# Score matmuls with 128 rows throughout, and chunked attention's query blocks in mixed order

## The chip, the cores and the metric

The kernel runs on one core of a Trainium2 chip. The metric is the device time of one execution in microseconds, from three runs (median). The profile is that of one further execution, taken by the hardware profiler.

## What is computed

Two transformer blocks on 1024 tokens of width 1024, in float32. The first block mixes tokens with three attentions side by side, then has cross attention over 256 memory tokens and a gated feed-forward layer. The second block has a pooling mixer and a sliding-window attention. The parts that matter here are the scores of three attentions with head size 64:

```python
# forget-gate attention ("fox"), 4 heads, causal
sc = einsum('bqhd,bkhd->bhqk', qb, k) * 64 ** -0.5
sc = sc + cum[q] - cum[k]          # cumulated log forget gates, per head
sc = where(k_pos <= q_pos, sc, -inf)

# chunked attention, 4 heads: chunks of 64 queries see their own and 8 chunks before
sc = einsum('bqhd,bkhd->bhqk', qc, kb) * 64 ** -0.5
sc = where(valid, sc + bias, -inf)

# sliding-window attention, 16 query heads on 2 key heads, window 128, with sinks
s = einsum('bnqhgd,bnkhd->bnhgqk', qn, kn) + pos_bias
```

Each is followed by a softmax over the keys and the product with the values. Every attention's output then goes through an RMS norm of its own.

## The kernel before

It is written by hand, engine by engine, with semaphores. A float32 operand of a large product is split into a high and a low part of type float32r, which TensorE takes in one pass each instead of the passes of plain float32: high x high, high x low, low x high (`product`, L489).

Attention is worked in units of one block of 128 queries (t = 0 to 7) and one head. `attention_pe` (L622) goes through the units with scores two units ahead: for each step it transposes the probabilities of unit u (`turn`, L647), makes the scores of unit u + 2 (`scores`, L637) and multiplies the transposed probabilities of unit u - 1 with the values (`weigh`, L659). VectorE takes the maximum of the scores (`maximum`, L693 or, with a bias, L697), ScalarE the exponential (L789); the two share the copies of the transposed probabilities (L714, L797). `att_mix` runs 96 units in one chain: 32 of latent attention (MLA), 32 of fox, 32 of chunked attention, each by query block in rising order, four heads to a block. `att_swa` runs 128 units of sliding-window attention and places between them, one product of 512 columns and three matmuls a step, the projection of the next heads' queries (`swa_beside`).

The scores of the 64-wide heads use a stacked operand: the query's high part in one half of the 128 partitions and its low part in the other (`fox_stack`, `chk_stack`, `swa_stack`), against the key's high part in both halves (`fox_khi`, `chk_khi`, `swa_khi`). That is one matmul of 128 rows. The query's high part against the key's low part (`fox_klo`, `chk_klo`, `swa_klo`) is a second one of 64 rows, since the low part lies in one half alone. Keys are taken in banks of 512 columns (`key_banks`, L828). Where the last bank has only 128 columns, plain float32 operands of 64 rows are used (`fox_q`, `fox_k`, `chk_q`, `chk_k`). In fox a third matmul in bfloat16 adds the forget gates: it takes the 32 rows of its head from `aug_q` and `aug_k`, into which the cumulated gates are laid in three parts. A block of fox ends with the causal mask, a bfloat16 matmul with the identity.

The splits of queries and keys for fox and chunked attention are made on GpSimd (POOL) while the attention before runs (L1191 to L1218), each waiting for the one before it through `half_ready`; TensorE waits for `HALVES` of them at the first unit of fox and for twice that at the first unit of chunked attention (L1388 to L1393). POOL then splits the strips of the next weights. For sliding window the key's high part is made on ScalarE (L1952), its low part on VectorE (L2362), the query stacks on POOL (L1230 to L1240).

Query block t of chunked attention has min(t, 4) + 1 tiles of 128 keys: 1, 2, 3, 4, and 5 for t = 4 to 7. Its outputs go to `ytok`, the sums of squares to `ystat` (L926), and after the last block the rows are scaled (POOL, L1224), transposed (L1405) and multiplied with the output weights.

Of the kernel before, what the change touches and what calls it, by code (L numbers as in the profile page):

```python
# [30 lines left out]
F32 = mybir.dt.float32  # L31
# [6 lines left out]
P = 128  # L38
# [23 lines left out]
HALVES = 5 * HEADS  # L62
# [37 lines left out]
N_CF = C_EPS + 2  # L100
# [5 lines left out]
def build(nc, dram, out):  # L106
    ctx = ExitStack()
    with ctx:
# [39 lines left out]
        def col(name, i=0, n=1):  # L148
# [8 lines left out]
                                              ("chk_klo", [P, HEADS // 2, T], F32R)])  # L157
# [4 lines left out]
        _, swa_klo, swa_bias, p3, pt3 = shared([("x_kept", [P, KEPT, T], F32), ("swa_klo", [P, T], F32R),  # L162
# [14 lines left out]
            ("v4", [P, HEADS, CHK_SPAN], F32), ("v5", [P, 2, T], BF16), ("v6", [P, T], F32), ("fox_norm", [P, 2, T], F32R)])  # L177
        (_, _, _, _, _, _, _, _, mem_raw, mem_hi, mem_lo) = shared([
# [23 lines left out]
        (swa_stack, swa_q, swa_kv, swa_z, swa_khi, swa_v, osb3) = shared([  # L202
            ("swa_stack", [P, 2, 2, T], F32R), ("swa_q", [P, 2, T], F32), ("swa_kv", [P, 2, T], F32),
            ("swa_z", [P, NK, T], F32), ("swa_khi", [P, 2, T], F32R),
            ("swa_v", [P, QT, P], F32), ("osb3", [P, HALF], F32)])
# [643 lines left out]
        def fox_stack(h, t, rows_of=slice(0, P)):  # L849
            if h < 2:  # L850
                return ring(split_hi, h)[rows_of, t * P:(t + 1) * P]
            return fox_rows[rows_of, t, fox_at + (h - 2) * P:fox_at + (h - 1) * P]
# [25 lines left out]
        for t in range(QT):  # L878
            q_tok = slice(t * P, (t + 1) * P)
            first = max(0, t - 4)  # L880
            for h in range(HEADS):
                r = slice(HD * (h % 2), HD * (h % 2) + HD)
# [114 lines left out]
        def stacks_done(tile, half, kv):  # L997
            return 2 * HALVES + 8 * tile + 4 * half + 2 * kv + 2

# [1545 lines left out]
```

## Time and profile before

| | us |
|---|---|
| median of three runs | 2717.97 |
| lowest and highest | 2709.69, 2726.29 |
| the profiled execution | 2709.43 |
| its span, first to last instruction | 2707.6 |
| TensorE matmul busy | 2602.9 (96%) |
| TensorE weight load busy | 2112.7 (78%) |
| VectorE busy | 1271.9 (47%) |
| ScalarE busy | 600.3 (22%) |
| GpSimd busy | 1108.2 (41%) |

The busy time of a matmul reaches from its start to the modelled end of its results; neighbours overlap, so what one costs the stream is read from start to start. TensorE's clock has two levels, 1.2 and 2.4 GHz; the granted clock is the share of full speed in a stretch.

### The profile page before, as it was taken

What the parts mean: (1) busy time and instruction counts of PE and PEld (TensorE: products, weight loads), DVE (VectorE), ACT (ScalarE), POOL (GpSimd) and SP (SyncE); (2) the same over time, 40 slices, a digit from 0 to 9 for tenths busy, and PEclk for the clock granted to TensorE, in tenths of its full rate; (3) what the DMA queues carried; (4) which work ended last, traced back from release to release, by engine and by line L of the source; (5) the groups of instructions that cost most, each with busy time, mean ns of one, the idle gap of its engine ahead of it and who ended that gap; (6) DMA issues with size and microseconds to landing.
All of it is one profiled execution on the core that took longest, in us unless ns stands there. A gap on an engine that the chain in (4) does not pass through costs nothing.

```text
span 2707.6 us, 30776 instructions
## 1 busy us (share of the span) xinstructions
PE 2602.9 (96%) x12086; PEld 2112.7 (78%) x12086; DVE 1271.9 (47%) x1526; ACT 600.3 (22%) x1189; POOL 1108.2 (41%) x507
## 2 busy tenths in 40 slices
PE   6999999999999999999999989999999999999987
PEld 5787777878777888888888867887878787777776
DVE  5247544343545353535352677342535272244465
ACT  3012444221232000000000332010101132344432
POOL 5533661014313444444444434443444443543345
PEclk9999998569999999999999999999999999999989
DMA  5411000011101223222321101111111113000033
GB/s 176 151 47 40 1 1 32 1 63 55 39 16 48 101 110 116 108 108 108 118 107 47 47 32 47 47 49 46 53 47 46 46 39 132 32 17 17 17 104 114
DMA packets 45935, 170.97 MB, mean 63 GB/s; under 512 B 4590, under 2 KB 9456, under 8 KB 40456
## 3 DMA queue, kind: packets, MB, share of 16 engines
q1 hardware_dynamic: 37832, 148.52, 15.6%
q10 hardware_dynamic: 8000, 21.01, 2.3%
q8 instruction: 72, 1.18, 0.2%
q14 instruction: 31, 0.25, 0.0%
HBM read 156.89 MB, written 12.57 MB: 63 GB/s over the span
## 4 chain that ended last, share of the span: by engine, by line
PE 87%; DVE 9%; issue 1%; ACT 1%; POOL 1%; DMA 0%; ACTq 0%; DVEq 0%; SPq 0%; POOLq 0%
PE ps L499 22%; PE ps L500 22%; PE ps L502 22%; PE ps L659 7%; PE ps L637 7%; PE ps L647 3%; DVE h_lo L438 1%; DVE sq_sum L342 1%; DVE h_lo L435 1%; DVE y_lo L2328 1%; PE ps L513 1%; PE ps L515 1%; PE ps L514 1%; DVE pool_b L2297 1%; DVE gated L427 0%
## 5 line engine op out<-in xcount | busy, mean ns | idle before, releaser
L1180 POOL TENSOR_TENSOR split_hi<-raw,cf 128x1024 fp32r<-128x1024 f32 x198 | 385.9, 1949 | 1258.0 <-PE ps L502 1121.5
L499 PE MATMUL ps<-h_hi,split_hi 128*128 128x512 f32 x2072 | 834.0, 402 | 34.1 <-DVE h_lo L435 8.0
L500 PE MATMUL ps<-h_lo,split_hi 128*128 128x512 f32 x2072 | 814.2, 393 | 0.0
L502 PE MATMUL ps<-h_hi,split_lo 128*128 128x512 f32 x2072 | 664.8, 392 | 0.0
L1182 POOL TENSOR_TENSOR split_lo<-raw,split_hi 128x1024 fp32r<-128x1024 f32 x198 | 558.5, 2821 | 15.6
L499 PEld LDWEIGHTS ps<-h_hi,split_hi 128*128 128x128 f32 x2072 | 394.1, 190 | 122.8 <-DVE h_lo L435 11.2
L502 PEld LDWEIGHTS ps<-h_hi,split_lo 128*128 128x128 f32 x2072 | 392.6, 189 | 83.8
L500 PEld LDWEIGHTS ps<-h_lo,split_hi 128*128 128x128 f32 x2072 | 394.4, 190 | 77.6 <-issue 1.9
L797 ACT COPY pt<-ps 128x256 f32<-128x256 f32 (+3 forms) x216 | 80.1, 371 | 317.2 <-PE ps L647 316.6
L697 DVE CUSTOM_DVE_ANT_0 p<-ps,swa_bias 128x256 f32<-128x256 f32 (+1 forms) x128 | 52.2, 408 | 204.4 <-PE ps L637 204.4
L499 PE MATMUL ps<-act_hi,split_hi 128*128 128x512 f32 x352 | 138.7, 394 | 3.9 <-DVE act_lo L2217 3.8
L647 PE MATMUL ps<-cf,p 128*128 128x128 f32 x712 | 134.7, 299 | 6.0 <-ACT p L789 3.2
L500 PE MATMUL ps<-act_lo,split_hi 128*128 128x512 f32 x352 | 137.8, 391 | 0.0
L2213 DVE TENSOR_TENSOR gated<-gated,ps 128x1024 f32<-128x1024 f32 x22 | 26.9, 1221 | 204.5 <-PE ps L502 204.5
L647 PEld LDWEIGHTS ps<-cf,p 128*128 128x128 f32 x712 | 101.5, 163 | 25.0 <-ACT p L789 8.6
L502 PE MATMUL ps<-act_hi,split_lo 128*128 128x512 f32 x352 | 108.8, 391 | 0.0
L499 PE MATMUL ps<-y_hi,split_hi 128*128 128x512 f32 x256 | 100.5, 393 | 8.5 <-DVE y_lo L2328 8.5
L1875 ACT ACTIVATE gated<-gated 128x1024 f32<-128x1024 f32 x22 | 23.3, 1061 | 379.2 <-DVE gated L2210 379.2
L342 DVE TENSOR_TENSOR sq_sum<-sq_sum,sq 128x1024 f32<-128x1024 f32 (+1 forms) x57 | 87.0, 1528 | 40.8 <-ACT sq L335 40.8
L500 PE MATMUL ps<-y_lo,split_hi 128*128 128x512 f32 x256 | 99.7, 389 | 0.0
L659 PE MATMUL ps<-vbc,pt 128*128 128x64 f32 x528 | 95.6, 342 | 0.0
L2229 DVE TENSOR_TENSOR xT<-xT,ps 128x1024 f32<-128x1024 f32 x48 | 58.6, 1220 | 78.4 <-PE ps L502 77.8
(323 smaller groups left out, 3589.3 us busy)
## 6 DMA issues: line engine op xcount, KB each, us to landing
raw<-in_strips SPq DMA_DIRECT2D x198, 512.0 KB, 3.4
ada_raw<-in_ada SPq DMA_DIRECT2D x32, 1024.0 KB, 5.6
xT<-in_xT SPq DMA_DIRECT2D x4, 1024.0 KB, 6.5
xT<-in_xT ACTq DMA_DIRECT2D x4, 1024.0 KB, 7.9
out_T<-out_sb SPq DMA_DIRECT2D x16, 256.0 KB, 2.2
x_spill_d<-xT ACTq DMA_DIRECT2D x1, 3584.0 KB, 11.9
xT<-x_spill_d ACTq DMA_DIRECT2D x2, 1792.0 KB, 8.8
swa_vec_d<-vbc ACTq DMA_DIRECT2D x1, 3064.0 KB, 19.3
```

Source lines behind the costliest of these rows:

```text
L342: dve.tensor_tensor(n["sq_sum"], n["sq_sum"], n["sq"], ALU.add).then_inc(n["sem"]["added"], 1)
L499: pe.matmul(acc[:, a:b], w_hi, hi[:, a:b], start=first, stop=False)
L500: pe.matmul(acc[:, a:b], w_hi, lo[:, a:b], start=False, stop=False)
L502: mm = pe.matmul(acc[:, a:b], w_lo, hi[:, a:b], start=False, stop=last)
L637: mm = pe.matmul(at[:, lo:hi], q, k, start=j == 0, stop=j == len(group) - 1)
L647: mm = pe.transpose(bank(4 + b % 2, P, j * P), probs[:, (b0 + j) * P:(b0 + j + 1) * P], ident)
L659: mm = pe.matmul(o, a["pt"][:, w % 4, j * P:(j + 1) * P], unit["values"][b0 + j], start=b0 + j == 0, stop=b0 + j == nblk - 1)
L697: dve.tensor_tensor_reduce(unit_probs(a, u), s, unit["bias"], 1.0, -3.0e38, ALU.add, ALU.max, rowmax[:, u:u + 1]).then_inc(a["biased"], 1)
L797: act.copy(a["pt"][:, w % 4, 0:nb * P], bank(4 + b % 2, nb * P)).then_inc(a["copied_act"], 1)
L1180: pool.tensor_tensor(hi, raw[:, r, :], ones[:, 0:1].to_broadcast([P, D]), ALU.mult).then_inc(hi_split, 1)
L1182: pool.tensor_tensor(lo, raw[:, r, :], rows(hi), ALU.subtract).then_inc(split_ready[r], 1)
L2229: dve.tensor_tensor(xT[:, o, :], xT[:, o, :], pair(2 + o % 2), ALU.add).then_inc(ffn_res, 1)
```

## The change

The key's low part is laid into both partition halves, so the second score matmul has 128 rows: it multiplies the whole query stack, high and low part, with the key's low part. (The product of the two low parts is added by this.) The plain float32 form for a last bank of 128 columns goes; such a bank is handled as the others. The forget-gate matmul takes all 128 rows: a copy of `aug_q` per head, in which the rows of the other heads are multiplied by zero (`fox_aug`, from four columns of ones and zeros in `cf`). Chunked attention works its query blocks in the order 4, 0, 5, 1, 6, 2, 7, 3; places in `ytok` and `ystat` follow.

POOL makes four more low parts and four masked copies for fox, four more low parts for chunked attention; VectorE makes two more low parts for sliding window.

```diff
-HALVES = 5 * HEADS
+FOX_HALVES = 7 * HEADS
+MIX_HALVES = FOX_HALVES + 6 * HEADS
+CHK_ORDER = [4, 0, 5, 1, 6, 2, 7, 3]
...
-C_ID, C_ONE, C_CNT, C_EPS = 0, P, 2 * P, 2 * P + 64
-N_CF = C_EPS + 2
+C_HEAD = C_EPS + 2
+N_CF = C_HEAD + HEADS
...
-                                              ("chk_klo", [P, HEADS // 2, T], F32R)])
+                                              ("chk_klo", [P, HEADS, T], F32R)])
...
+            ("fox_aug", [P, HEADS, T], BF16), ("fox_kr", [P, 2, T], F32R)])
...
         def fox_klo(h):
-            return fox_raw[:, h // 2, :]
+            return fox_raw[:, h, :] if h < 2 else fox_kr[:, h - 2, :]
...
-                r = slice(HD * (h % 2), HD * (h % 2) + HD)
-                f = slice(32 * h, 32 * h + 32)
-                sc = []
-                for lo, hi in key_banks(n):
-                    if hi - lo < 2 * P:
-                        sc.append([(fox_q[r, h // 2, q_tok], fox_k[r, h // 2, lo:hi], lo, hi)])
-                    else:
-                        sc.append([(fox_stack(h, t), fox_khi(h)[:, lo:hi], lo, hi),
-                                   (fox_stack(h, t, r), fox_klo(h)[r, lo:hi], lo, hi)])
-                    sc[-1].append((aug_q[f, q_tok], aug_k[f, lo:hi], lo, hi))
+                sc = [[(fox_stack(h, t), fox_khi(h)[:, lo:hi], lo, hi),
+                       (fox_stack(h, t), fox_klo(h)[:, lo:hi], lo, hi),
+                       (fox_aug[:, h, q_tok], aug_k[:, lo:hi], lo, hi)] for lo, hi in key_banks(n)]
...
-        for t in range(QT):
+        for t in CHK_ORDER:
...
-                    if hi - lo < 2 * P:
-                        sc.append([(chk_q[r, h // 2, q_tok], chk_k[r, h // 2, k_tok], lo, hi)])
-                    else:
-                        sc.append([(chk_stack[:, h, q_tok], chk_khi[:, h, k_tok], lo, hi),
-                                   (chk_stack[r, h, q_tok], chk_klo[r, h // 2, k_tok], lo, hi)])
+                    sc.append([(chk_stack[:, h, q_tok], chk_khi[:, h, k_tok], lo, hi),
+                               (chk_stack[:, h, q_tok], chk_klo[:, h, k_tok], lo, hi)])
...
+        def mix_tokens(g):
+
+            return CHK_ORDER[g % QT] if g >= 2 * QT else g % QT
...
-                    sc = [(stack[:, q_tok], swa_khi[:, kv, k_tok], 0, n), (stack[r, q_tok], swa_klo[r, k_tok], 0, n)]
+                    sc = [(stack[:, q_tok], swa_khi[:, kv, k_tok], 0, n), (stack[:, q_tok], swa_klo[kv][:, k_tok], 0, n)]
...
+                low(fox_klo(h)[other, :], fox_k[r, h // 2, :], fox_khi(h)[r, :])
                 low(fox_klo(h)[r, :], fox_k[r, h // 2, :], fox_khi(h)[r, :])
+            for h in range(HEADS):
+                half_split(pool.tensor_tensor(fox_aug[:, h, :], aug_q[:, :],
+                                              cf[:, C_HEAD + h:C_HEAD + h + 1].to_broadcast([P, T]), ALU.mult))
...
-                low(chk_klo[r, h // 2, :], chk_k[r, h // 2, :], chk_khi[r, h, :])
+                low(chk_klo[r, h, :], chk_k[r, h // 2, :], chk_khi[r, h, :])
+                low(chk_klo[other, h, :], chk_k[r, h // 2, :], chk_khi[r, h, :])
...
                 if u == QT * HEADS:
-                    eng.wait_ge(half_ready, HALVES)
+                    eng.wait_ge(half_ready, FOX_HALVES)
...
                 if u == 2 * QT * HEADS:
                     eng.wait_ge(chk_ready, 2)
-                    eng.wait_ge(half_ready, 2 * HALVES)
+                    eng.wait_ge(half_ready, MIX_HALVES)
...
-                dve.scalar_tensor_tensor(out=swa_klo[r, :], in0=swa_kv[r, 0, :], scalar=shift_out[r, 0:1],
-                                         in1=rows(swa_khi[r, kv, :]), op0=ALU.add, op1=ALU.subtract).then_inc(kv_klo, 1)
+                for rows_of in range(2):
+                    dve.scalar_tensor_tensor(out=swa_klo[kv][HD * rows_of:HD * rows_of + HD, :], in0=swa_kv[r, 0, :],
+                                             scalar=shift_out[r, 0:1], in1=rows(swa_khi[r, kv, :]),
+                                             op0=ALU.add, op1=ALU.subtract).then_inc(kv_klo, 1)
...
+    cf[:, C_HEAD:C_HEAD + HEADS] = np.arange(P)[:, None] // 32 == np.arange(HEADS)[None, :]
```

## Rows read from the trace of the kernel before

**Rows 1.** The page: granted clock in 40 equal slices (tenths), and the chain by engine.

```profile
PEclk9999998569999999999999999999999999999989
...
PE 87%; DVE 9%; issue 1%; ACT 1%; POOL 1%; DMA 0%; ACTq 0%; DVEq 0%; SPq 0%; POOLq 0%
```

**Rows 2.** Busy time by stretch: length, each engine (instructions), granted clock, DMA share, GB/s.

```profile
350.50:446.00 95.50, 95.50 (x611) 68.85 (x610) 42.67 (x72) 41.06 (x107) 41.51 (x20) 1.00 0.00 1
...
458.50:571.50 113.00, 112.94 (x430) 93.99 (x429) 44.22 (x121) 29.80 (x88) 8.35 (x4) 0.50 0.03 11
...
2326.00:2561.00 235.00, 234.42 (x1293) 184.17 (x1293) 96.58 (x413) 108.81 (x377) 101.46 (x75) 0.99 0.06 19
2561.00:2602.00 41.00, 31.70 (x147) 24.87 (x147) 24.77 (x62) 16.61 (x50) 4.25 (x2) 0.79 0.04 13
```

**Rows 3.** Timeline of TensorE in chunked attention: start, length, instruction, count.

```profile
504.23 0.78 PE L637 MATMUL ps<-chk_khi,chk_stack 128*128 128x512 f32 x1
504.94 0.79 PE L637 MATMUL ps<-chk_klo,chk_stack 64*128 64x512 f32 x1
...
506.09 2.39 PE L659 MATMUL ps<-vbc,pt 128*128 128x64 f32 x10
...
509.20 0.78 PE L637 MATMUL ps<-chk_khi,chk_stack 128*128 128x512 f32 x1
```

**Rows 4.** Timeline of TensorE in fox, a unit of two banks.

```profile
431.69 0.48 PE L637 MATMUL ps<-split_lo,split_hi 128*128 128x512 f32 x1
432.10 0.50 PE L637 MATMUL ps<-fox_raw,split_hi 64*128 64x512 f32 x1
432.53 0.38 PE L637 MATMUL ps<-aug_k,aug_q 32*128 32x512 bf16 x1
432.85 0.49 PE L637 MATMUL ps<-split_lo,split_hi 128*128 128x512 f32 x1
...
433.69 0.38 PE L637 MATMUL ps<-aug_k,aug_q 32*128 32x512 bf16 x1
434.01 0.23 PE L637 MATMUL ps<-cb 128*128 128x128 bf16 x1
...
436.44 0.48 PE L637 MATMUL ps<-fox_norm,fox_rows 128*128 128x512 f32 x1
```

**Rows 5.** Timeline of TensorE in sliding window, one unit with its projection products.

```profile
2440.77 0.36 PE L637 MATMUL ps<-swa_khi,swa_stack 128*128 128x256 f32 x1
2441.06 0.38 PE L637 MATMUL ps<-swa_klo,swa_stack 64*128 64x256 f32 x1
2441.38 0.66 PE L659 MATMUL ps<-swa_v,pt 128*128 128x64 f32 x4
2441.84 0.48 PE L499 MATMUL ps<-h_hi,split_hi 128*128 128x512 f32 x1
2442.16 0.39 PE L500 MATMUL ps<-h_lo,split_hi 128*128 128x512 f32 x1
2442.39 0.39 PE L502 MATMUL ps<-h_hi,split_lo 128*128 128x512 f32 x1
...
2442.76 0.36 PE L637 MATMUL ps<-swa_khi,swa_stack 128*128 128x256 f32 x1
```

**Rows 6.** Timeline of TensorE in the block of two key tiles, chunked attention.

```profile
457.60 0.36 PE L637 MATMUL ps<-chk_khi,chk_stack 128*128 128x256 f32 x1
...
458.87 0.56 PE L637 MATMUL ps<-chk_khi,chk_stack 128*128 128x256 f32 x1
```

**Rows 7.** Timeline of TensorE in cross attention.

```profile
744.31 0.60 PE L637 MATMUL ps<-mem_k,cross_q 128*128 128x256 f32 x2
744.75 0.61 PE L659 MATMUL ps<-mem_v,pt 128*128 128x128 f32 x4
```

**Rows 8.** Timeline of POOL: the last preparation for fox and for chunked attention.

```profile
311.56 2.35 POOL L1172 TENSOR_TENSOR fox_raw<-fox_k,fox_norm 64x1024 fp32r<-64x1024 f32 x1
...
400.46 2.35 POOL L1172 TENSOR_TENSOR chk_klo<-chk_k,chk_khi 64x1024 fp32r<-64x1024 f32 x1
```

More of the change, by code:

```diff
@@ L161, in build @@
         mraw, kv_hi, kv_lo = shared([("mraw", [P, 6, T], F32), ("kv_hi", [P, T], F32R), ("kv_lo", [P, T], F32R)])
-        _, swa_klo, swa_bias, p3, pt3 = shared([("x_kept", [P, KEPT, T], F32), ("swa_klo", [P, T], F32R),
+        _, swa_klo0, swa_bias, p3, pt3 = shared([("x_kept", [P, KEPT, T], F32), ("swa_klo0", [P, T], F32R),
                                                 ("swa_bias", [P, SWA_HEADS, 2 * P], F32), ("p3", [P, 4, 2 * P], F32),
@@ L177, in build @@
             ("v4", [P, HEADS, CHK_SPAN], F32), ("v5", [P, 2, T], BF16), ("v6", [P, T], F32), ("fox_norm", [P, 2, T], F32R)])
+        _, _, _, _, _, _, _, _, fox_aug, fox_kr = shared([
+            ("a1", [P, HEADS, MEM], F32), ("a2", [P, 2, HALF], F32), ("a3", [P, QT, HALF], F32),
+            ("a4", [P, HEADS, CHK_SPAN], F32), ("a5", [P, 2, T], BF16), ("a6", [P, T], F32), ("a7", [P, T], F32), ("a8", [P, T], F32),
+            ("fox_aug", [P, HEADS, T], BF16), ("fox_kr", [P, 2, T], F32R)])
         (_, _, _, _, _, _, _, _, mem_raw, mem_hi, mem_lo) = shared([
@@ L201, in build @@
             ("pool_b", [P, T + 16], F32)])
-        (swa_stack, swa_q, swa_kv, swa_z, swa_khi, swa_v, osb3) = shared([
+        (swa_stack, swa_q, swa_kv, swa_z, swa_khi, swa_v, osb3, swa_klo1) = shared([
             ("swa_stack", [P, 2, 2, T], F32R), ("swa_q", [P, 2, T], F32), ("swa_kv", [P, 2, T], F32),
             ("swa_z", [P, NK, T], F32), ("swa_khi", [P, 2, T], F32R),
-            ("swa_v", [P, QT, P], F32), ("osb3", [P, HALF], F32)])
+            ("swa_v", [P, QT, P], F32), ("osb3", [P, HALF], F32), ("swa_klo1", [P, T], F32R)])
+        swa_klo = (swa_klo0, swa_klo1)
         _, gated_early = shared([("w12", [P, 2, 2, T], F32R), ("gated_early", [P, 2, HALF], F32R)])
@@ L847, in ring, with fox_stack @@
             return tensor[:, r, :, :].rearrange("p a n -> p (a n)")
-        def fox_stack(h, t, rows_of=slice(0, P)):
+        def fox_stack(h, t):
             if h < 2:
-                return ring(split_hi, h)[rows_of, t * P:(t + 1) * P]
-            return fox_rows[rows_of, t, fox_at + (h - 2) * P:fox_at + (h - 1) * P]
+                return ring(split_hi, h)[:, t * P:(t + 1) * P]
+            return fox_rows[:, t, fox_at + (h - 2) * P:fox_at + (h - 1) * P]
         def fox_khi(h):
@@ L881, in build @@
             for h in range(HEADS):
-                r = slice(HD * (h % 2), HD * (h % 2) + HD)
                 n = (t + 1 - first) * P
@@ L910, in build @@
                     h = 2 * tile + kv
-                    r = slice(HD * kv, HD * kv + HD)
                     stack = swa_stack[:, tile % 2, kv, :]
-                    sc = [(stack[:, q_tok], swa_khi[:, kv, k_tok], 0, n), (stack[r, q_tok], swa_klo[r, k_tok], 0, n)]
+                    sc = [(stack[:, q_tok], swa_khi[:, kv, k_tok], 0, n), (stack[:, q_tok], swa_klo[kv][:, k_tok], 0, n)]
                     swa_units.append(unit(
@@ L920, in build @@
         att_mix = attention_plan(mix_units, HEADS, 2, p1, pt1, None)
-        att_mix["dst"] = lambda g: ytok[:, g % QT, mix_columns[g // QT][0]:mix_columns[g // QT][1]]
+        att_mix["dst"] = lambda g: ytok[:, mix_tokens(g), mix_columns[g // QT][0]:mix_columns[g // QT][1]]
         def mixed_square(act, g):
@@ L929, in mixed_square @@
             need(act, y_sq, g - 1)
-            act.activation(sq[:, (g % 2) * HALF:(g % 2) * HALF + b - a], ytok[:, g % QT, a:b], ACT.Square,
-                           accum_out=ystat[:, 0, g:g + 1]).then_inc(y_sq, 1)
+            at = QT * (g // QT) + mix_tokens(g)
+            act.activation(sq[:, (g % 2) * HALF:(g % 2) * HALF + b - a], ytok[:, mix_tokens(g), a:b], ACT.Square,
+                           accum_out=ystat[:, 0, at:at + 1]).then_inc(y_sq, 1)
         def mixed_root(act, p0, p1):
@@ L997, in stacks_done @@
         def stacks_done(tile, half, kv):
-            return 2 * HALVES + 8 * tile + 4 * half + 2 * kv + 2
+            return MIX_HALVES + 8 * tile + 4 * half + 2 * kv + 2
         def gated_high(act, n):
@@ L1629, in swa_ready @@
                     eng.wait_ge(kv_k, 4)
-                    eng.wait_ge(kv_klo, 2)
+                    eng.wait_ge(kv_klo, 4)
                     eng.wait_ge(kv_v, 1)
```

## The prediction

> **What bounds the kernel now.** I read the page first. The chain that ended last is 87% TensorE, 9% VectorE, and the row of the granted clock shows nine tenths or more everywhere but in three slices before a quarter of the span, where it is 0.8, 0.5 and 0.6 [rows 1]. So time is to be found in what TensorE does, and in that clock. Next I cut the span into stretches at the attention stages [rows 2]. Forget-gate (fox) attention runs from 350.5 to 446 at a clock of 1.00. Chunked attention starts at 446 and from 458.5 to 571.5 it has 0.50, that is 1.2 GHz, with TensorE busy for 112.9 of 113 us: it never idles, it is slow. Sliding-window attention (2326 to 2561) has 0.99. In each of the three TensorE is busy throughout, VectorE and ScalarE under half of the time, so every microsecond taken from TensorE's stream there is off the end.
>
> Last I read the starts of single matmuls in the timeline, since durations overlap and starts don't. Three units are enough.
>
> - A chunked unit of 640 keys, half clock [rows 3]: high part of the first 512 keys at 504.23, low part (64 rows) at 504.94, then the last 128 keys (64 rows, two passes), weighting from 506.09, the next unit's high part at 509.20. Period 4.97 us, the same in all 16 units of 640 keys.
> - A fox unit of two 512-column banks, full clock [rows 4]: 128-row high part to 64-row low part 0.41, low part to 32-row forget-gate matmul 0.43, that one to the next 128-row one 0.32, to the mask 0.32; period 4.75.
> - A sliding-window unit [rows 5]: 128-row high part to 64-row low part 0.29, low part to 128-row weighting 0.32, for 256 columns each; period 1.99 (2440.77 to 2442.76), the three 512-column products of the projection among it.
>
> **What a start ought to cost.** In [rows 5] the projection's product L500, 512 columns of split operands with 128 rows on both sides of it, gives way to the next after 0.23 us, so 512 split columns cost 0.21 to 0.23 and 256 about 0.11. Its forerunner L499 takes 0.32, and it is the first split matmul after weighting in plain f32: a change of type costs about 0.10. Cross attention has 128-row operands alone, and [rows 7] show its two plain passes over 256 columns done in 0.44 us, with weighting right behind: no step there. Against this, high to low part costs 0.18 too much in sliding window, low part to weighting 0.21; in fox the steps cost 0.20, 0.22, 0.11 and 0.11 too much. Wherever the number of rows changes, time is lost; where it stays, it isn't. That is the first gain the edit can have. But up to 0.10 of each first step may be the change of type, not of rows.
>
> The Trainium skill, in TensorEngine Tiling (Array Packing), Key Properties, says that a change of tiling mode drains TensorE; by that all of the excess would go. It speaks for the edit. The Trainium skill, in TensorE: Matmul & The Clock Gate, Part 3, says the reverse for padding: weight loads overlap running matmuls only when the row groups differ. What by that rule would follow is the second rival below; the 0.23 of [rows 5] and the 0.44 of [rows 7], both between 128-row neighbours, speak against it.
>
> **The change, part by part.**
>
> 1. *Fox.* A unit of two banks has the steps high-low, low-gate, gate-high, high-low, low-gate, gate-mask: 0.20, 0.22, 0.11, 0.21, 0.22, 0.10, together 1.06. I take off 0.10 for the type at the first step and 0.11 for gate to high, leaving 0.85. Units of one bank have the first two and the last: 0.52, less 0.10, 0.42. There are 16 of each: 13.6 + 6.7 = 20. Bounds: 12 (another 0.10 at each bank's first low part and gate step) and 25 (all of it). The gate matmul has 128 rows instead of 32, its columns are the same; I cost that at nothing.
> 2. *Sliding window.* 0.18 + 0.21 = 0.39 a unit, less the type's share of the first step, 0.39 - 0.12 = 0.27. There are 128 units: 34. Bounds 26 (the second step alone) and 50. What comes next there is ScalarE, busy 108.8 of 235 us [rows 2]: at 1.72 us a unit it is still under 60%.
> 3. *Chunked.* In [rows 3] 10 weighting passes and 5 transposes take 3.11 us, 0.207 each at half clock, so 0.104 at full. At full clock and with rows alike a 640-key unit is 15 x 0.104 = 1.56, two splits of 512 (0.44), two of 128 that cost no less than such a pass (0.21), and 0.10 for the type: 2.31, I take 2.33. 16 units save 16 x (4.97 - 2.33) = 42. Of the 113 us at half clock 16 x 4.97 = 79.5 are these; the other 33.5 (blocks of 3 and 4 key tiles, the end) would halve and save 16.8, but in short units the chain of score, maximum, exponential and transpose is longer than TensorE's work, so I take 13. The blocks of one and two tiles ran at full clock: 1. The new order puts seven borders between large and small blocks, where transposes wait for a score issued two short steps before: 0.4 us each, 3 against. Sum 53. VectorE is next: its 44.2 us busy [rows 2] would be three quarters of the 60 us left. Bounds 41 (borders and short units cost 12 more) and 59 (the 33.5 halve, borders cost 1).
> 4. *Behind it.* The transposes after attention would run at full clock too, ahead of a chain over VectorE, ScalarE and POOL that keeps its length; 0 to 4 us, I take 2.
> 5. *Work added.* POOL prepares fox until 313.9 and chunked until 402.8 [rows 8]. Fox gets four low parts (2.35 each) and four masks of the forget rows over 128x1024, each between one and two such parts in length (twice the rows, half the bytes written): 19 to 28 us, so it ends by 342 at most, before TensorE asks at 350.5. Chunked gets 9.7 more, ends at 412.5, and is asked for near 446 - 20 = 426. Covered; without cover the first would cost its whole 19. On VectorE two more low parts of 64x1024 stand ahead of the copy of the values, which TensorE waits for only before the fourth strip of the query projection, a strip of 48 products (11 us) later: nothing, and 2.6 at most without that cover. POOL's next strips come after a semaphore of fox's last weighting, and wait for no one here.
>
> Sum: 20 + 34 + 53 + 2 = 109. The profiled execution took 2709.4 (span 2707.6 and 1.8 around it), so 2600; the median of the runs shown is 2718.0, 0.3% above, which gives 2609. I say 2608.
>
> **Does the clock hold?** This decides half of the sum. What the row before the fall shows: it fell at 458.5, soon after fox's last weighting, when only units of one and two key tiles were left [rows 6], each start of a high part 1.27 us after the last, with little in between. Fox has small blocks too, at 350 to 365, kept at full clock with the gate and mask matmuls in each. Sliding window lost the clock in a stall at 2561 and again at 2580 and had it back while still running such units, all in the 0.79 of [rows 2]; chunked attention never had it back, with 64-row matmuls in a third of its scores. The new order opens with a 640-key block and puts never more than one small block between large ones, and all operands have 128 rows. Both go the right way. Nothing in the trace shows a chunked unit at full clock for longer than 12 us, so I can't be sure.
>
> The Trainium skill, in TensorE: Matmul & The Clock Gate, Part 1, has the clock drop when TensorE has been idle. By it chunked attention, idle for 0.1 us of 113, would have stayed at full clock; the trace does not agree.
>
> **The rivals.**
>
> - *The clock falls again and stays.* For it: the block of one key tile is sparser than anything that is there now. Then fox 20 and sliding window 34 stay, and chunked saves only its steps between rows. In [rows 3] high to low is 0.71 and low to weighting 1.15, where 0.43 and 0.86 are due at half clock: 0.57, less 0.15 for types, 0.4 x 16 and 4 for the others: 10. 2718 - 64 = 2654. If it falls late or comes back, in between.
> - *The steps are not due to rows* but to weight loads that 128-row neighbours can't hide, or to types. The clock holds; a 640-key unit is half of what it is, 2.48: chunked saves 50, fox and sliding window nothing. 2718 - 52 = 2666. For it: the type changes at most of the same places. Against it: 256 columns in sliding window go from low part to weighting in 0.32, yet L500 with more columns and loads of the same size takes 0.23. This is also what the rule of the Trainium skill in TensorE: Matmul & The Clock Gate, Part 3, on weight loads would give.
> - *Slower: the clock falls in fox.* Fox's small blocks get shorter for TensorE while the chain of score, maximum and exponential stays as long, so TensorE waits in them. If that makes the clock fall near 355 as it fell at 458.5, and nothing brings it back before sliding window, fox takes 2 x 75.5 = 151 us, 55 more than now; chunked saves 10 and sliding window its lower bound of 26: 2718 + 55 - 36 = 2737. It decides once the low clock in fox lasts some 36 us and the gains of chunked stay out. Against it: fox holds 1.00 throughout now.
> - *No effect:* the edit doesn't do what it says, rows make no step and the clock falls: 2705 to 2720.
>
> **How the numbers follow.** Forecast 0.62, clock falls 0.16, not rows 0.14, fox falls 0.04, no effect 0.04. The forecast's own range is 2588 to 2632: bounds of items 1 and 2 together -16 to +21, of chunked -6 to +12, which seldom meet. To leave out no more than 2 in 10 it must reach over the first rival and touch the second: 2588 to 2666. A measurement of this kernel can tell about 0.5% from no change. Faster by more than that: 0.62 + 0.16 + 0.14 = 0.92; within 0.04; slower 0.04.
>
> **What would show it.** The granted clock in chunked attention 1.00 with a period near 2.3 for 640 keys (2.5: VectorE is the bound; 4.6: the clock fell). Sliding-window period 1.72; 1.99 kills the first gain. Fox's two-bank unit of 4.75 at 3.9; low to gate at 0.21 to 0.23. No wait of TensorE on POOL at the first unit of fox or chunked. I am wrong if the one-tile blocks bring the clock down, or if high to low stays at 0.29 in sliding window with 128 rows on both.

## The result and the profile after

The changed kernel takes 2588.7 us (median of 4 executions, 2582.2 to 2590.9) against 2722.1 for the kernel before (4 executions beside it, 2709.7 to 2727.1): a ratio of 0.951, 95% interval 0.947 to 0.955. The forecast was 2608, its range 2588 to 2666. All four executions of the kernel before lie here in the slower of the two clusters that the table under The experiments shows; the ratios given there leave out the executions of either kernel in which the clock was low for long. The profiled execution has a span of 2586.7 us, 120.9 less than before.

The page of the changed kernel, in answer to [rows 1]: the granted clock in 40 slices, and the chain by engine.

```profile
PEclk9999999899999999999999989999999999999998
...
PE 85%; DVE 10%; ACT 2%; issue 2%; POOL 1%; DMA 0%; ACTq 0%; DVEq 0%; SPq 0%; POOLq 0%
```

The dip to 0.5 and 0.6 before a quarter of the span has shrunk to one slice of 0.8. By stretch (columns as in [rows 2]); the second to the fourth are chunked attention:

```profile
348.50:426.20 77.70, 77.09 (x603) 66.35 (x610) 42.85 (x73) 40.97 (x107) 51.00 (x24) 1.00 0.01 1
426.20:451.00 24.80, 21.73 (x179) 20.65 (x178) 17.37 (x50) 12.39 (x38) 8.47 (x4) 1.00 0.25 86
451.00:468.00 17.00, 17.00 (x83) 16.71 (x81) 8.01 (x28) 5.64 (x20) 0.00 (x0) 0.50 0.00 1
468.00:501.00 33.00, 32.19 (x258) 30.41 (x256) 24.56 (x73) 18.45 (x53) 0.00 (x0) 1.00 0.00 1
```

Fox takes 77.6 us from its first score to the first one of chunked attention (95.5 before, from 350.89 to 446.35). Chunked attention takes 74.6 to the end of its last weighting (125.1 before, from 446.35 to 571.43). The clock did fall again, at 451, but came back at 468; before, it stayed low from 458.5 to the end of the stage.

TensorE's timeline, start and length, a chunked unit of 640 keys at full clock, in answer to [rows 3]:

```profile
487.19 0.47 PE L645 MATMUL ps<-chk_khi,chk_stack 128*128 128x512 f32 x1
487.50 0.40 PE L645 MATMUL ps<-chk_klo,chk_stack 128*128 128x512 f32 x1
487.74 0.23 PE L645 MATMUL ps<-chk_khi,chk_stack 128*128 128x128 f32 x1
...
487.91 1.28 PE L667 MATMUL ps<-vbc,pt 128*128 128x64 f32 x10
489.02 0.72 PE L655 MATMUL ps<-cf,p 128*128 128x128 f32 x5
489.50 0.48 PE L645 MATMUL ps<-chk_khi,chk_stack 128*128 128x512 f32 x1
```

The period is 2.31 (4.97 before, at half clock). A fox unit of two banks, in answer to [rows 4]:

```profile
418.24 0.48 PE L645 MATMUL ps<-fox_norm,fox_rows 128*128 128x512 f32 x1
418.55 0.40 PE L645 MATMUL ps<-fox_kr,fox_rows 128*128 128x512 f32 x1
418.79 0.39 PE L645 MATMUL ps<-aug_k,fox_aug 128*128 128x512 bf16 x1
418.83 0.58 PE L645 MATMUL ps<-fox_norm,fox_rows 128*128 128x512 f32 x1
419.25 0.40 PE L645 MATMUL ps<-fox_kr,fox_rows 128*128 128x512 f32 x1
419.48 0.39 PE L645 MATMUL ps<-aug_k,fox_aug 128*128 128x512 bf16 x1
...
422.13 0.48 PE L645 MATMUL ps<-fox_norm,fox_rows 128*128 128x512 f32 x1
```

Period 3.89 (4.75 before). A sliding-window unit, in answer to [rows 5]:

```profile
2330.79 0.36 PE L645 MATMUL ps<-swa_khi,swa_stack 128*128 128x256 f32 x1
2330.99 0.28 PE L645 MATMUL ps<-swa_klo,swa_stack 128*128 128x256 f32 x1
2331.11 0.55 PE L667 MATMUL ps<-swa_v,pt 128*128 128x64 f32 x4
2331.47 0.47 PE L507 MATMUL ps<-h_hi,split_hi 128*128 128x512 f32 x1
...
2332.39 0.36 PE L645 MATMUL ps<-swa_khi,swa_stack 128*128 128x256 f32 x1
```

Period 1.60 (1.99 before): high to low 0.20 instead of 0.29, low to weighting 0.12 instead of 0.32, weighting to the product 0.36 instead of 0.46.

So the 120.9 us of the two traces are: fox 17.8, chunked attention 50.4, sliding window 49.9 (276.2 from its first score to its last weighting before, 226.3 after; 0.39 x 128 is 50), and 2.3 ahead of fox, of which the clock accounts for under 2 us: it was low for about 3 us longer there before.

**Why the clock fell in the changed kernel.** Three views show one moment. VectorE, the scaling of a token block (L950) and the next unit's bias and maximum (L705):

```profile
445.48 2.62 DVE L950 TENSOR_SCALAR xT<-xT,ystat 128x512 f32<-128x512 f32 x1
448.02 0.81 DVE L705 CUSTOM_DVE_ANT_0 p<-ps,chk_bias 128x640 f32<-128x640 f32 x1
```

POOL, the last of four operations that split two weight strips:

```profile
445.45 2.37 POOL L1184 TENSOR_TENSOR split_lo<-raw,split_hi 128x1024 fp32r<-128x1024 f32 x1
```

TensorE, the transposes behind it (in brackets: idle before, and who ended it):

```profile
450.04 0.77 PE L655 MATMUL ps<-cf,p 128*128 128x128 f32 x5 [1.84 <-ACT p L797]
```

The same scaling takes 0.48 in each of the next seven blocks. Here it stands from POOL's start (445.45) to just behind POOL's end (447.82); so the maximum, the exponential and TensorE are late, TensorE idles 1.84 us, and a microsecond later its clock falls. This became the theory to test. Against it stood the forecast's own picture, that 64 rows and the sparse small blocks decide on the clock.

### The profile page after: what moved, and what is told of

The parts are those of the page before. It is cut to its first block, busy times and chain, and to the rows that moved or that the text cites. A ratio compares the mean times of both kernels' runs of the same rounds, so it can differ in the third digit from the quotient of the medians.

```text
span 2586.7 us, 30782 instructions
## 1 busy us (share of the span) xinstructions
PE 2475.3 (96%) x12078; PEld 2050.2 (79%) x12086; DVE 1282.4 (50%) x1528; ACT 599.2 (23%) x1189; POOL 1136.5 (44%) x519
## 4 chain that ended last, share of the span: by engine, by line
PE 85%; DVE 10%; ACT 2%; issue 2%; POOL 1%; DMA 0%; ACTq 0%; DVEq 0%; SPq 0%; POOLq 0%
PE ps L507 23%; PE ps L508 22%; PE ps L510 22%; PE ps L667 6%; PE ps L645 4%; PE ps L655 3%; DVE h_lo L446 2%; DVE sq_sum L350 1%; DVE h_lo L443 1%; DVE y_lo L2335 1%; PE ps L521 1%; PE ps L523 1%; PE ps L522 1%; DVE pool_b L2304 1%; DVE tmp L435 0%
## 5 line engine op out<-in xcount | busy, mean ns | idle before, releaser
L655 PE MATMUL ps<-cf,p 128*128 128x128 f32 x712 | 124.3, 280 | 11.7 <-ACT p L797 8.5
L705 DVE CUSTOM_DVE_ANT_0 p<-ps,swa_bias 128x256 f32<-128x256 f32 (+1 forms) x128 | 52.2, 408 | 145.7 <-PE ps L645 144.9
L655 PEld LDWEIGHTS ps<-cf,p 128*128 128x128 f32 x712 | 89.5, 147 | 33.8 <-ACT p L797 19.5
L2343 DVE SCALAR_TENSOR_TENSOR xT<-ps,adav,xT 128x1024 f32<-128x1024 f32 x32 | 41.1, 1283 | 103.5 <-PE ps L510 103.5
```

The source lines that it names most:

```text
L655: mm = pe.transpose(bank(4 + b % 2, P, j * P), probs[:, (b0 + j) * P:(b0 + j + 1) * P], ident)
L705: dve.tensor_tensor_reduce(unit_probs(a, u), s, unit["bias"], 1.0, -3.0e38, ALU.add, ALU.max, rowmax[:, u:u + 1]).then_inc(a["biased"], 1)
```

## The experiments

Each was compared with the kernel before on its own chip, in three groups on three chips. Execution times first, because they changed the question:

| kernel | executions, us |
|---|---|
| before, beside the first comparison | 2710, 2718, 2726, 2727 |
| before, first group | 2653, 2666, 2666, 2667, 2668, 2704, 2718 |
| before, second group | 2654, 2655, 2659, 2660, 2662, 2667, 2712, 2717, 2722, 2727, 2727 |
| before, third group | 2660, 2665, 2667, 2668, 2676, 2704, 2710, 2717, 2718, 2726, 2727 |
| changed, both times | 2578, 2580, 2581, 2582, 2582, 2588, 2589, 2590, 2590, 2591 |
| scaling later, both times | 2577, 2578, 2579, 2580, 2582, 2582, 2582, 2583, 2583, 2583 |
| rows only, both times | 2578, 2580, 2581, 2581, 2583, 2584, 2584, 2584, 2585, 2586 |
| order only, both times | 2588, 2588, 2589, 2589, 2590, 2591, 2592, 2592, 2593 |
| chunked as before | 2590, 2591, 2593, 2642 |
| window only | 2607, 2609, 2609, 2623, 2666, 2668 |

The times of the kernel before lie in two clusters, 2653 to 2676 with a mean clock of 0.975 to 0.986 and 2704 to 2727 with 0.953 to 0.965: it loses the clock for long in some executions and not in others.

### Chunked attention, part by part

**Rows only:** rising order again, 128 rows.

```diff
-CHK_ORDER = [4, 0, 5, 1, 6, 2, 7, 3]
+CHK_ORDER = [0, 1, 2, 3, 4, 5, 6, 7]
```

> The changed kernel with the blocks of chunked attention back in rising order (0, 1, ..., 7); all operands keep 128 rows. Theory A (128 rows keep or bring back TensorE's clock, the order adds little): the clock is below 0.6 for at most 25 us, chunked attention takes 72 to 82 us, the kernel 2586 to 2597 us. Theory B (it is the order that keeps the clock): the clock falls in the small blocks as in the kernel before and stays at 0.50 to the end of the stage, which takes about 110 us (125 before, less some 10 for steps between row counts), the kernel 2615 to 2630 us.

Measured: 2582.5 (2580.2 to 2584.1), ratio 0.970 (0.966 to 0.973). Chunked attention takes 68.3 us; the clock is low for 3 us only (0.52 from 444 to 447), after a stall of 1.7. That is near theory A and below its 72 to 82 us and 2586 to 2597: the order wasn't needed.

**Order only:** 64 rows as before (the short last bank in plain f32), mixed order.

```diff
...
-                    sc.append([(chk_stack[:, h, q_tok], chk_khi[:, h, k_tok], lo, hi),
-                               (chk_stack[:, h, q_tok], chk_klo[:, h, k_tok], lo, hi)])
+                    if hi - lo < 2 * P:
+                        sc.append([(chk_q[r, h // 2, q_tok], chk_k[r, h // 2, k_tok], lo, hi)])
+                    else:
+                        sc.append([(chk_stack[:, h, q_tok], chk_khi[:, h, k_tok], lo, hi),
+                                   (chk_stack[r, h, q_tok], chk_klo[r, h, k_tok], lo, hi)])
```

> The changed kernel with the operands of chunked attention as before (low part 64 rows, last 128 keys in plain f32 on 64 rows), in the mixed order. Theory A (rows keep the clock): it falls and stays at 0.50, the stage takes 105 to 122 us, the kernel 2620 to 2636. Theory B (order): the clock comes back as in the changed kernel (0.50 for about 17 us of the stage), the stage takes 74.6 us and 24 to 28 units times 0.3 to 0.4 us for the steps, about 84, the kernel 2596 to 2600.

Measured: 2588.5, ratio 0.972 (0.967 to 0.977); an execution of 5529 us at a mean clock of 1.00, twice the time, is left out here and in the table, and nothing explains it. The stage takes 74.4 us at clock 1.00. That is nearer to theory B, whose stage of 84 us was too long: it had a fall of 17 us in it, and there is none. So neither part alone lets the clock fall for long, and neither theory had the other's result.

**Chunked as before:** both of these edits together (rising order, and the 64-row operands of the diff just shown).

> The changed kernel with chunked attention wholly as before: 64-row operands and rising order; fox and sliding window keep their 128 rows. If the stages add up, the whole of what chunked attention gave is lost: stage about 125 us, kernel 2589 + 50 = 2639 (2632 to 2646). If fox or sliding window took part of their gain from chunked attention (by the clock), their stages are longer than 77.6 and 200 us too.

Measured: 2590.5 to 2592.7 in three executions and 2641.6 in the fourth; expected was 2639 in all. The profile is of one of the three. Chunked attention, stretch as in [rows 2]:

```profile
426.30:501.00 74.70, 74.35 (x513) 61.61 (x512) 49.36 (x147) 36.26 (x110) 8.66 (x4) 1.00 0.08 29
```

This is the code that ran at 0.50 in the profile of before. At full clock the stage takes 74.6 us instead of 125.1: the fall costs 50.5, and it isn't fixed by the code. (Fox is the new one here; in window only, below, with fox as before as well, the stage takes 74.6 at 1.00 too.)

**Window only:** both of these edits and fox as before too (its diff is shown below), so that in TensorE's work only the sliding window is new.

> The kernel before with nothing new but the 128-row low part of sliding-window attention (fox and chunked attention as before, rising order). Executions with full clock: 2586 + 18 + 8 = 2612 (or before's fastest 2653 less 50 = 2603). Theory F (the layout of fox and chunked attention decides on the clock): long falls as in the kernel before in at least a third of the executions, those at 2650 to 2675. Theory H (it is the chip and the moment alone): as rare as in the other kernels of this call.

Measured: 2607.3 to 2609.2 in three executions, 2623.4 in one, 2666.4 and 2668.1 in two. Theory F expected long falls in at least a third and got 2 of 6, just that; their times of 2666 and 2668 lie where it said. The unit of 640 keys with 64 rows, at full clock:

```profile
481.42 0.47 PE L645 MATMUL ps<-chk_khi,chk_stack 128*128 128x512 f32 x1
481.83 0.50 PE L645 MATMUL ps<-chk_klo,chk_stack 64*128 64x512 f32 x1
482.17 0.38 PE L645 MATMUL ps<-chk_k,chk_q 64*128 64x128 f32 x2
482.48 1.33 PE L667 MATMUL ps<-vbc,pt 128*128 128x64 f32 x10
...
484.11 0.48 PE L645 MATMUL ps<-chk_khi,chk_stack 128*128 128x512 f32 x1
```

Period 2.69 against 2.31 with 128 rows: 0.38 a unit is what the rows and the split form of the last bank give here together, 0.10 of it from high to low (0.41 to 0.31).

**The changed kernel once more**, without an edit, in the same group.

> The changed kernel once more, beside the kernel before on the same chip. The profile of chunked attention as before (in a kernel with the new fox and sliding window) showed the clock at 1.00 all through that stage, so the fall of the kernel before isn't fixed by the code. Theory E (whether the clock falls for long in the kernel before differs from execution to execution, by about 50 us; the changed kernel only ever loses it for short): times of before lie apart in groups from 2650 to 2727, those of the changed kernel all between 2580 and 2592. Theory G (both kernels have it alike, the first comparison met the changed kernel in luck): some executions of the changed kernel stand 15 to 50 us above the others.

Measured: 2581.7 (2578.0 to 2590.2), ratio 0.971 (0.968 to 0.973), with before at 2654 to 2667 in six executions and at 2712 to 2727 in five. Theory E. In its profile the clock fell at 453 (0.50 from 454 to 467) after a stall of 1.69 that ended at 451.76, as in the first one.

**Rows only and order only once more**, to count long falls.

> Chunked attention with 128 rows in rising order once more, for the number of executions. So far the kernels with 64-row operands in rising order (before, and the two experiments that left chunked attention as it was) lost the clock for 50 us or more in 14 of 32 executions, all kernels with either part of the edit in 0 of 33, 4 of them of this kernel. Theory I (the rows prevent the long fall): 0 of 6 here, 2578 to 2592. Theory J (the order alone does): about 3 of 6 at 2610 to 2630, since a long fall would cost 16 units of 640 keys 2.3 us each.

Measured: 2577.8 to 2586.1, none of 6 with a long fall; the profile has the stage at 66.8 us and clock 1.00.

> Chunked attention with 64-row operands in the mixed order once more. Theory I (the rows prevent the long fall): about 3 of 6 executions at 2630 to 2645. Theory J (the order does): 0 of 6, all at 2584 to 2600. Both 0 here and 0 in the kernel with 128 rows alone: either part is enough.

Measured: 2588.5 to 2592.9, none of 6.

Theory I expected three long falls here, theory J three in the other kernel; there is none in either. In all: 64 rows in rising order fell for long in 20 of 43 executions (before 17 of 33, chunked as before 1 of 4, window only 2 of 6), 128 rows in rising order in 0 of 10, 64 rows in mixed order in 0 of 9, every kernel with both parts in 0 of 33. By these counts either part is enough. One thing they don't settle: the kernels with one part alone all have the new fox, and with the new fox and chunked attention as before there are only 4 executions, one of them with the fall; whether fox has a share isn't shown. At full clock the order saves 0.1 us (74.57 to 74.43 in the stage), and the rows and the split form save 8.7 behind that (74.43 to the 65.74 of scaling later, below).

### The stall

**Scaling later:** the first token block is scaled a group of units later, together with the second.

```diff
-            if g >= 2 * QT:
+            if g == 2 * QT + 1:
+                mixed_scale(dve, 0, 0)
+            if g > 2 * QT:
                 mixed_scale(dve, 0, g - 2 * QT)
```

> The changed kernel, only that VectorE scales the first token block of the first columns (128x512 in place in xT) one group of units later, together with the second, so that the operation doesn't run while POOL splits the strips. Theory C (POOL blocks this operation, it makes the stall of 1.84 us, and the stall brings the clock down at 451): every such operation takes 0.48 us, no wait of TensorE near 450 is above 0.9 us, the clock stays 1.00, the stage takes about 74.6 - 8.5 = 66 us, the kernel 2578 to 2582. Theory D (the sparse block of one key tile brings the clock down, the stall is beside the point): 0.48 us as well, but the clock falls near 451 all the same and the stage is shorter by 1 to 2 us, the kernel 2586 to 2588.

Measured: 2582.7 (2578.9 to 2583.5), ratio 0.969 (0.965 to 0.973). The two first scalings take 0.87 together, the longest wait of TensorE near there is 0.9, the clock is 1.00 throughout and the stage takes 65.7 us. Theory C, up to one point: the kernel's time lies only 2.5 us under the 2585.2 that the ten executions of the changed one average.

> The changed kernel with VectorE's scaling moved behind POOL's splits, once more, now in 6 executions beside the others of this call. Theory C (the stall made by POOL brings the short fall near 451, 8 us in about half of the executions of the changed kernel): all 6 at 2577 to 2584, median 2581; none at 2588 to 2591 as 5 of the 10 of the changed kernel. Theory D (the fall comes without the stall too): one to three of them at 2588 to 2591.

Measured: 2580.9 (2576.6 to 2583.3), ratio 0.968 (0.965 to 0.970). Chunked attention in its profile:

```profile
425.80:491.60 65.80, 63.12 (x515) 60.01 (x513) 47.62 (x147) 36.52 (x110) 8.47 (x4) 1.00 0.10 33
```

None of 10 executions lies at 2588 or above, where 5 of 10 of the changed kernel do. Their averages are 2581.0 and 2585.2. By the averages it is 0.16% faster than the changed kernel, less than a single comparison tells.

How firm is the link between stall and fall? Six profiles with the mixed order or 128 rows have a stall of 1.35 to 1.84 us there: in four the clock fell behind it (for 17, 17, 14 and 3 us), in two it did not. In the five such profiles without the stall it never fell. These counts and the ten executions of scaling later speak for it that the stall brings the fall, not every time; eleven profiles are too few for more. The stall by itself costs little: gate on 32 rows (below) has one of 1.82 and no fall, and its stage takes 67.3 us, between the 65.7 without either and the 74.6 with both. So the stall costs 1.6 and the fall 7.3.

### Sliding window and fox

**Window with 64 rows:**

```diff
+r = slice(HD * kv, HD * kv + HD)
-sc = [(stack[:, q_tok], swa_khi[:, kv, k_tok], 0, n), (stack[:, q_tok], swa_klo[kv][:, k_tok], 0, n)]
+sc = [(stack[:, q_tok], swa_khi[:, kv, k_tok], 0, n), (stack[r, q_tok], swa_klo[kv][r, k_tok], 0, n)]
```

> The changed kernel with the low part of sliding-window attention on 64 rows again (the key part's own half and the same half of the query stack). Theory A (steps between row counts, 0.39 us a unit as the two profiles show): period 1.99 again, the kernel 2586 + 50 = 2636. By the forecast's term (0.27 a unit, the rest being a change of type that the rows can't mend): 2586 + 34 = 2620.

Measured: 2640.5 (2634.2 to 2649.5), 59 above the median of the changed kernel in the same group (2581.7); fastest above fastest it is 56. TensorE:

```profile
2403.00 0.36 PE L645 MATMUL ps<-swa_khi,swa_stack 128*128 128x256 f32 x1
2403.29 0.38 PE L645 MATMUL ps<-swa_klo,swa_stack 64*128 64x256 f32 x1
2403.61 0.66 PE L667 MATMUL ps<-swa_v,pt 128*128 128x64 f32 x4
2404.07 0.48 PE L507 MATMUL ps<-h_hi,split_hi 128*128 128x512 f32 x1
...
2404.99 0.36 PE L645 MATMUL ps<-swa_khi,swa_stack 128*128 128x256 f32 x1
```

Period 1.99 again, with nothing changed but the rows: theory A, 0.39 a unit; the forecast's 34 us are refuted. From first score to last weighting the stage takes 282.8 us here, 276.2 before, and 228.3 to 228.4 in eight of the twelve profiles with 128 rows. So the rows are worth 48 us of the whole stage, and the other 6.6 are the clock's. Near the end of this stage every profile has stalls of TensorE and a low clock behind them. In this one the first stall is of 2.61 us (until 2481.98), and the clock is at half for 37 us behind it:

```profile
2482.00:2517.00 35.00, 31.23 (x99) 23.85 (x99) 16.28 (x40) 10.72 (x34) 4.27 (x2) 0.50 0.04 15
```

In before and in those eight it is at half for 17 us there, in the first profile of the changed kernel for 10. Since before has 64 rows as well, the rows alone don't explain the 37; why it is so long is open.

The weight loads tell more about the step. PEld in this profile:

```profile
2402.97 0.19 PEld L645 LDWEIGHTS ps<-swa_khi,swa_stack 128*128 128x128 f32 x1
2403.29 0.18 PEld L645 LDWEIGHTS ps<-swa_klo,swa_stack 64*128 64x128 f32 x1
2403.61 0.52 PEld L667 LDWEIGHTS ps<-swa_v,pt 128*128 128x128 f32 x4
```

and in the changed kernel, for the unit shown above:

```profile
2330.76 0.19 PEld L645 LDWEIGHTS ps<-swa_khi,swa_stack 128*128 128x128 f32 x1
2330.87 0.19 PEld L645 LDWEIGHTS ps<-swa_klo,swa_stack 128*128 128x128 f32 x1
2330.99 0.53 PEld L667 LDWEIGHTS ps<-swa_v,pt 128*128 128x128 f32 x4
```

With 128 rows on both sides the low part's load starts 0.12 us ahead of its matmul (2330.99), while the high part's matmul runs, and the first load of weighting likewise. With 64 rows the load starts only together with its matmul (2403.29), and so does the first one of weighting behind it (2403.61). Whether the late load is what holds the matmul up, or both wait for the same thing, the traces don't tell.

By chance the same profile shows the blocked scaling the other way round. VectorE:

```profile
445.48 0.48 DVE L951 TENSOR_SCALAR xT<-xT,ystat 128x512 f32<-128x512 f32 x1
```

and POOL, which came 0.13 later:

```profile
445.61 2.59 POOL L1185 TENSOR_TENSOR split_lo<-raw,split_hi 128x1024 fp32r<-128x1024 f32 x1
```

Now the scaling has its 0.48 and POOL's operation takes 2.59 instead of 2.35: whichever starts first goes first, the other waits. That chance of 0.1 us decides whether TensorE stalls.

**Fox as before:** 64-row low part, 32-row gate, last banks of 128 columns in plain f32; POOL's extra low parts and masks for fox go as well.

```diff
-                sc = [[(fox_stack(h, t), fox_khi(h)[:, lo:hi], lo, hi),
-                       (fox_stack(h, t), fox_klo(h)[:, lo:hi], lo, hi),
-                       (fox_aug[:, h, q_tok], aug_k[:, lo:hi], lo, hi)] for lo, hi in key_banks(n)]
...
+                    if hi - lo < 2 * P:
+                        sc.append([(fox_q[r, h // 2, q_tok], fox_k[r, h // 2, lo:hi], lo, hi)])
+                    else:
+                        sc.append([(fox_stack(h, t), fox_khi(h)[:, lo:hi], lo, hi),
+                                   (fox_stack(h, t)[r, :], fox_klo(h)[r, lo:hi], lo, hi)])
+                    sc[-1].append((aug_q[f, q_tok], aug_k[f, lo:hi], lo, hi))
...
```

> The changed kernel with fox attention as before (low part 64 rows, gate 32 rows, single banks in plain f32 on 64 rows). If the stages add up: 17.8 us more, the kernel 2603 to 2606. If fox's 128 rows also carry the clock through the chunked stage behind it, the clock falls there for long in some executions and they stand near 2640.

Measured: 2603.4 (2598.0 to 2612.8), 21.7 over the changed kernel; the fastest 20 over the fastest. None near 2640. Its profile shows the clock fall inside fox, with TensorE busy to the last and no stall:

```profile
424.50:439.50 15.00, 15.00 (x66) 10.81 (x65) 4.54 (x6) 6.42 (x11) 0.00 (x0) 0.64 0.00 1
```

Within it the clock is at half from 425 to 435 and again from 439 to 442. This costs about 6 us (fox 101.5 instead of 95.5). It is the second fall without a stall, after the one at 458.5 in the kernel before, and again it comes among matmuls of 64 rows, here with 32-row ones between them.

**Gate on 32 rows**, all else of the changed kernel:

```diff
...
-                       (fox_aug[:, h, q_tok], aug_k[:, lo:hi], lo, hi)] for lo, hi in key_banks(n)]
+                       (aug_q[f, q_tok], aug_k[f, lo:hi], lo, hi)] for lo, hi in key_banks(n)]
```

> The changed kernel with the forget-gate matmul of fox back on 32 rows, its neighbours on 128. Theory A (a step wherever the rows change): low to gate goes from 0.23 to about 0.43 and gate to the next high part or mask from 0.23 to 0.33, 0.3 us for each of 48 gate matmuls, fox 13 to 14 us longer (91 to 92), the kernel near 2595. If only the step down from 128 to 64 rows cost anything: 77 to 79 us as in the changed kernel.

Measured: 2590.8, one execution; fox 87.1 us. The two-bank unit:

```profile
421.95 0.48 PE L645 MATMUL ps<-split_lo,split_hi 128*128 128x512 f32 x1
422.26 0.40 PE L645 MATMUL ps<-fox_raw,split_hi 128*128 128x512 f32 x1
422.59 0.39 PE L645 MATMUL ps<-aug_k,aug_q 32*128 32x512 bf16 x1
422.91 0.50 PE L645 MATMUL ps<-split_lo,split_hi 128*128 128x512 f32 x1
423.25 0.40 PE L645 MATMUL ps<-fox_raw,split_hi 128*128 128x512 f32 x1
...
426.33 0.48 PE L645 MATMUL ps<-fox_norm,fox_rows 128*128 128x512 f32 x1
```

Low to gate is 0.33 instead of 0.24 to 0.23, and gate to the next 0.32. From the first low part to the second it is 0.99 instead of 0.70, so three starts come 0.10 later each: the gate's, the next one, and the one behind that. The period is 4.38 instead of 3.89. The stage is 9.5 us longer, not 13 to 14: theory A has the right mechanism and too large a size, since I took the step out of 64 rows (0.43 in [rows 4]) for one out of 128.

## Why the prediction was right, and where it wasn't

The time is inside the range and under the forecast's 2608 by 19 us. Between the two profiles the sum of 109 became 120.9: sliding window gave 16 more, fox and chunked attention 2 to 3 less each, 2.3 came from ahead of fox, and the 2 behind chunked attention came to 0.3. That is 12 of the 19. The other 7 are the step from a profile to the median: I went from 2600 to 2608 by the 0.3% that the kernel before showed, and the changed kernel shows none (2588.5 in the profile, 2588.7 the median). A slip in the bounds moved nothing: -16 to +21 is of the gain, -6 to +12 for chunked attention is of the time. Point by point:

- **What bounds the kernel.** Right: TensorE busy in all three stretches. "It never idles, it is slow" held; what it hid is that the profile before was one of two ways in which that kernel runs. That all of its executions I had seen ran that way was chance.
- **Fox, 20.** Measured 17.8, two-bank period 3.89 (3.9 forecast). From the last one-bank unit's mask to the end of the stage it is 65.65 before (from 380.70) and 52.55 after (from 373.70), so the two-bank units gave 13.1 (13.6 forecast) and the one-bank units the other 4.7, where I had 6.7. The split by experiment: 9.5 from the gate's rows, the other 8.3 from the low part's rows and the split form of the last banks.
- **Sliding window, 34.** The term that was mis-sized: 50, of which 48 are the rows' and 2 the clock's (at half for 10 us near the end of the stage instead of 17). I put high to low at 0.06 of gain; it was 0.09. Low to weighting at 0.21; it was 0.20. The third I hadn't priced at all: weighting to the first product (0.46 in [rows 5]) lost 0.10 as well, so a 64-row matmul also delays the second start behind it. The upper bound of 50 was just enough.
- **Chunked, 53.** The sum is right (50.4) with the wrong parts. Period 2.33 forecast, 2.31 measured. But "the clock holds at 1.00" failed: the stall and 17 us at 0.50 cost 8.9 (74.6 against 65.7 in the profiles that have neither), 1.6 and 7.3 of it. What the sum called the gain is 50.5 of clock, 8.8 of rows, form and order, and 8.9 given back. That the last two cancel, so that the sum came out right, is luck. The borders: I allowed 3 us for seven; the waits at them sum to 2.4 in the profile of scaling later and to 3.5 here.
- **Behind it, 2.** It gave 0.3 (14.34 us from the last weighting to the end of the next long wait before, 14.01 after). The transposes didn't run at full clock: 16 took 3.35 us instead of 3.68, at 0.66 between 500.8 and 505.2. The wait for VectorE behind them went from 4.19 to 4.76.
- **Work added, 0.** Right, and the cover held. POOL's new masks and its last low parts:

```profile
323.68 7.82 POOL L1214 TENSOR_TENSOR fox_aug<-aug_q,cf 128x1024 bf16<-128x1024 bf16 x4
...
404.45 4.78 POOL L1174 TENSOR_TENSOR chk_klo<-chk_k,chk_khi 64x1024 fp32r<-64x1024 f32 x2
```

  They end at 331.5 (342 at most, I said) and 409.2 (412.5), and TensorE waits for neither. A mask took 1.96 us, less than one low part and not one to two. What I overlooked is POOL's next work: the two weight strips, which "wait for no one here". They don't, but VectorE waits for them. They start 11 to 14 us behind chunked attention's first score in every trace. Before (458 to 467) the scaling took 1.74 there and TensorE, with 64-row scores of small blocks still to do, covered it, as in chunked as before (1.49) and order only (1.09). With 128 rows TensorE is through sooner, and stalls in either order.
- **"Does the clock hold?"** The sign I named for being wrong came true in its word: the one-tile block stands just ahead of where the clock fell. Not in its mechanism: the sparse block alone doesn't do it (scaling later has the same block and 1.00); the stall is what the counts point to. And the sentence "chunked attention never had it back, with 64-row matmuls in a third of its scores" was an argument from one execution.
- **The rivals.** The clock falls and stays: no, in none of the 33 executions with both parts. Steps not due to rows: refuted by the window with 64 rows, where rows alone bring 1.99 back. The Trainium skill, in TensorE: Matmul & The Clock Gate, Part 3, has weight loads overlap running matmuls only where the row groups differ; by it 128-row neighbours would be the slow ones, and they are the fast ones, 0.12 against 0.32, with the load 0.12 ahead of its matmul under the running one (window with 64 rows). Slower by a fall in fox: the changed fox held 1.00 in every profile, but the old fox did lose the clock once. No effect: no.

**What remains open.** Why 64 rows in rising order lose the clock with TensorE busy, and why either part of the edit stops it. No run told a cause there, only the counts. Nor is it known why one execution of order only took 5529 us, or why the clock stayed low for 37 us in window with 64 rows. With before at its full clock the change is worth 3% (0.971), not 5%.

## What to carry to other kernels

Keep the number of partition rows alike in neighbouring matmuls: a 64-row one among 128-row ones costs 0.4 us at full clock (0.10 ahead of it, 0.20 behind it, 0.10 one start later), a 32-row one 0.2 on average (9.5 us for 48 of them), and filling rows with zeros or a second copy cost nothing on TensorE here (a gate matmul of 128 rows gives way after 0.23, like the low part). Before a stage at half clock is priced, several executions of the kernel belong beside the profile: a gain of 50 us was here in 17 of 33 executions and not in the other 16. And when the order of blocks is changed, look at what every other engine does beside the new border.

## What the runs showed of the hardware

- A step between 128 and 64 rows costs 0.09 to 0.10 us into the shorter matmul, 0.20 out of it and another 0.10 at the start behind that; for 32 rows in bf16 it is about 0.10 at each of the three.
- Between 128-row neighbours the weight load starts under the running matmul, 0.12 us ahead of its own; where the rows change from 128 to 64 or back it starts together with its own (2403.29 and 2403.61 in window with 64 rows).
- VectorE's scaling of 128x512 f32 within SBUF (0.48) and POOL's operation over 128x1024 f32 (2.35) exclude each other: the scaling took 2.62, 2.46, 2.49, 2.58, 2.60 and 2.15 when POOL was first, while VectorE's operations that read PSUM ran at their 0.82 beside it. The Trainium skill, in SBUF — State Buffer, SBUF: two separate sides, describes it as a shared port pair held for a whole instruction by whichever engine starts first; both orders seen here agree.
- The granted clock fell with TensorE busy without a gap (458.5 in before, 425 in fox as before) and came back at 468 in the changed kernel while the same kind of units ran on at half speed.
- Behind the stalls near the end of sliding window the clock was at half for 17 us in most profiles, for 10 in two and for 37 in one.
- The same program on the same chip lost the clock for long in about half of its executions, 50 us apart.
